# Second mixer's latent heads: values as the stationary operand, turned probabilities moving, two heads in two column strips

## What is computed

```python
q = (rmsnorm(c_q, q_norm) @ w_uq).reshape(B, S, H, MLA_NOPE + MLA_ROPE)     # H = 16, S = 256
kv = (rmsnorm(c_kv, kv_norm) @ w_ukv).reshape(B, S, H, MLA_NOPE + MLA_V)   # MLA_V = 64
...
    s = (einsum('bqhd,bkhd->bhqk', qn, k_nope)
         + einsum('bqhr,bkr->bhqk', qr, k_rope)) * scale
    p = jax.nn.softmax(jnp.where(kpos[None, :] <= qpos[:, None], s, NEG), axis=-1)
    o = einsum('bhqk,bkhd->bqhd', p, v)
return o.reshape(B, S, H * MLA_V) @ w_o
```

## Time and profile before

| what | us |
|---|---|
| median of three runs (lowest to highest) | 1389.64 (1388.46 to 1389.67) |
| the profiled execution's own time | 1388.37 |
| its span | 1386.6 |
| TensorE busy, DVE busy, ACT busy in the span | 1375.7, 901.8, 741.9 |
| granted clock of TensorE, mean | 0.998 |
| the latent heads, from the end of step 15's transposes to the first matmul of the projection | 630.4 to 654.5 |

### The profile page before, as it was taken

One profiled execution on the slowest core, in us unless ns is written; L12 is line 12 of the kernel. 1 busy time (PEld: TensorE's weight loads), 2 busy tenths in 40 slices (PEclk: granted clock), 3 DMA queues, 4 the chain that ended last, 5 costly groups with the idle time before them and its releaser, 6 DMA issues.

```text
span 1386.6 us, 21310 instructions
## 1 busy us (share of the span) xinstructions
PE 1375.7 (99%) x8246; PEld 1219.9 (88%) x8246; DVE 901.8 (65%) x1156; ACT 741.9 (54%) x921; POOL 60.8 (4%) x97
## 2 busy tenths in 40 slices
PE   9999999999999999999999999999999999999997
PEld 8999989888888888899888888888889999888886
DVE  6565798565566656776666667666657767666566
ACT  7566665343464444558554445545445467544444
POOL 1000010100010000010200000000000002100000
PEclk9999999999999999999999999999999999999999
DMA  9543432255455555561565554755555400555552
GB/s 373 183 173 122 174 131 92 91 209 202 154 183 187 201 187 182 180 210 37 209 249 182 189 203 155 272 182 182 183 199 194 153 32 5 224 184 195 197 182 91
DMA packets 34717, 240.16 MB, mean 173 GB/s; under 512 B 3994, under 2 KB 4138, under 8 KB 6880
## 3 DMA queue, kind: packets, MB, share of 16 engines
q1 hardware_dynamic: 32928, 232.50, 47.0%
q0 software_dynamic: 1296, 6.15, 1.2%
q10 hardware_dynamic: 432, 0.66, 0.1%
HBM read 237.16 MB, written 1.08 MB: 172 GB/s over the span
## 4 chain that ended last, share of the span: by engine, by line
PE 97%; DMA 1%; DVE 1%; ACT 1%; issue 0%; POOL 0%; POOLq 0%; ACTq 0%; DVEq 0%
PE ps L750 22%; PE ps L720 16%; PE ps L722 16%; PE ps L721 16%; PE ps L758 12%; PE ps L1056 3%; PE ps L1030 2%; PE ps L1040 2%; PE ps L1382 1%; DMA raw<-in_stream 1%; PE ps L3048 1%; PE ps L662 1%; PE ps L3054 1%; PE ps L3251 1%; PE ps L846 1%; PE ps L1376 0%
## 5 line engine op out<-in xcount | busy, mean ns | idle before, releaser
L427 DVE TENSOR_TENSOR low<-raw,high 128x2048 fp32r<-128x2048 f32 x210 | 478.6, 2281 | 230.0 <-ACT high L416 229.7
L416 ACT ACTIVATE high<-raw 128x2048 fp32r<-128x2048 f32 (+1 forms) x212 | 401.9, 1898 | 75.4 <-PE ps L722 70.6
L750 PE MATMUL ps<-nt,high 128*128 128x512 f32 x1344 | 319.9, 390 | 0.0
L750 PEld LDWEIGHTS ps<-nt,high 128*128 128x128 f32 x1344 | 249.0, 188 | 49.7
L758 PEld LDWEIGHTS ps<-nt,low 128*128 128x128 f32 x1344 | 167.5, 189 | 3.6
L758 PE MATMUL ps<-nt,low 128*128 128x256 f32 x1344 | 168.6, 283 | 0.0
L720 PE MATMUL ps<-high,hth 128*128 128x512 f32 x320 | 124.5, 389 | 0.0
L721 PE MATMUL ps<-low,hth 128*128 128x512 f32 x320 | 124.5, 389 | 0.0
L722 PE MATMUL ps<-high,htl 128*128 128x512 f32 x320 | 124.5, 389 | 0.0
L720 PE MATMUL ps<-nt,high 128*128 128x256 f32 x392 | 111.5, 285 | 0.0
L722 PE MATMUL ps<-nt,low 128*128 128x256 f32 x392 | 110.7, 282 | 0.0
(11 more groups left out here) (441 smaller groups left out, 1995.7 us busy)
## 6 DMA issues: line engine op xcount, KB each, us to landing
raw<-in_stream SPq DMA_DIRECT2D x214, 1024.0 KB, 4.8
late<-in_first SPq DMA_DIRECT2D x4, 512.0 KB, 5.7
late<-in_w POOLq DMA_DIRECT2D x1, 2048.0 KB, 11.3
scr<-bias_by_distance POOLq DMA_DIRECT2D x1, 2048.0 KB, 14.0
raw<-in_stream SPq DMA_DIRECT2D x2, 512.0 KB, 7.7
x<-in_x SPq DMA_DIRECT2D x1, 1024.0 KB, 11.9
scr<-in_mem SPq DMA_DIRECT2D x1, 1024.0 KB, 15.2
scr<-scr SPq DMA_DIRECT2D x8, 128.0 KB, 2.4
```

The costliest lines, as they stand in the source:

```text
L416: nc.scalar.activation(high_of(t, slice(0, n)), raw[t % SLOTS][:, 0:n], ACT.Copy).then_inc(w_high, 1)
L427: nc.vector.tensor_tensor(low_of(t, slice(0, n)), raw[t % SLOTS][:, 0:n], high_of(t, slice(0, n)).bitcast(F32), ALU.subtract).then_inc(w_l ...
L750: last = nc.tensor.matmul(r3(bank, 2), w[:, k, P * j:P * j + P], nt[:, :, k, :], start=first and k == 0, stop=not first and k == KC - 1, s ...
```

## The change

For the latent heads alone, and nowhere else:

- The product with the values is made for two heads together once for each pair (`values_by_features`, in even steps). The values of a head, 128 keys by 64 features without the column of ones, are stationary; the turned probabilities move, 256 columns for the first 128 keys and 128 columns for the second. The output has features on the partitions: the even head in partitions 0 to 63, the odd head in 64 to 127, so that the two heads take two column strips of the array. The turned blocks are put in another order in PSUM for that (`turned_probs_at`), and there are four buffers for the copies in place of two, since both heads of a pair have to be there.
- The sums come from the exponentials (`accum_out`). From the third pair on the exponentials wait for `at_read`, since there are three buffers of sums.
- DVE takes the reciprocal of the sums of a pair spread over 64 columns each, so of 128x256 elements with tokens on the partitions, into `ml_yt` (`at_shares`). TensorE transposes this in two blocks of 128x128, right behind the products of the pair. DVE then copies the turned shares from PSUM, and multiplies the output in PSUM with them into `ml_yt`.
- The transposes of `pe_y` fall away for these heads. `act_y` and `dve_y` read `ml_yt`.

```diff
+            def values_by_features(p):
+                for a in (2 * p, 2 * p + 1):
+                    pe.wait_ge(at_copied[a % 2], a // 2 + 1)
+                pe.wait_ge(at_read, 2 * (p - 1))
+                for kt in range(TT):
+                    for a in (2 * p, 2 * p + 1):
+                        half = slice(64 * (a % 2), 64 * (a % 2) + 64)
+                        last = nc.tensor.matmul(heads_out(p)[half, P * kt:S], UNITS[a]["v"][kt][:, 0:MLA_V],
+                                                ml_p[a % 4][:, S * kt:S + P * kt], start=kt == 0, stop=kt == 1,
+                                                skip_group_check=True)
+                last.then_inc(at_out, 1)
+                pe.wait_ge(at_shares, p - MLA0 // 2 + 1)
+                for t in range(TT):
+                    last = nc.tensor.transpose(heads_shares(p)[:, P * t:P * t + P], ml_yt[:, slot_of(p), P * t:P * t + P], ident)
...
+                last.then_inc(at_out, 1)
...
-                if first <= a - 3:
+                if first <= a - 3 and by_features(a - 3):
+                    if (a - 3) % 2:
+                        values_by_features((a - 3) // 2)
+                elif first <= a - 3:
                     values(a - 3)
...
+                    if by_features(a) and a >= first + RING:
+                        act.wait_ge(at_read, 2 * ((a - RING) // 2) + 2)
...
+                            last = nc.scalar.activation(at_s[b][:, c], src[:, c], ACT.Exp, scale=-1.0,
+                                                        bias=at_nm[r][:, t:t + 1],
+                                                        accum_out=at_sums[a // 2 % 3][:, at:at + 1])
...
+                if not odd and first <= a - 5 < first + n and by_features(a - 5):
+                    yt = ml_yt[:, slot_of(p - 1), :]
+                    dve.wait_ge(at_out, 2 * (p - 1) + 2)
+                    ch.link(nc.vector.tensor_copy(yt, heads_shares(p - 1)))
+                    nc.vector.tensor_tensor(yt, heads_out(p - 1), yt, ALU.mult).then_inc(at_read, 2)
...
+                if odd and by_features(a - 2) and first <= a - 2 < first + n:
+                    q = (a - 2) // 2
+                    if q - MLA0 // 2 >= 4:
+                        dve.wait_ge(turn_low, y_turned("mly", (q - MLA0 // 2 - 4) // 2))
+                    dve.wait_ge(at_exp, a - 1)
+                    nc.vector.reciprocal(ml_yt[:, slot_of(q), :].rearrange("p (t u d) -> p t u d", t=TT, u=2),
+                                         by_unit(at_sums[q % 3]).rearrange("p u t -> p t u").unsqueeze(3)
+                                         .broadcast_to([P, TT, 2, 64])).then_inc(at_shares, 1)
```

More of the change, by code:

```diff
@@ L931, in build, with by_features, slot_of, probs_at @@
         neg_sink = tiny(SW_H)
+        at_shares = s_("at_shares")
+        ml_p = [at_p[0], at_p[1], ml["y"][:, 1024:1536], ml["y"][:, 1536:2048]]
+        ml_yt = r3(ml["y"][:, 0:1024], 4)
+        def by_features(a):
+            return MLA0 <= a < MLA0 + MLA_H
+        def slot_of(p):
+            return (p - MLA0 // 2) % 4
+        def probs_at(a):
+            return ml_p[a % 4] if by_features(a) else at_p[a % 2]
+        def turned_probs_at(a, c):
+            return ((P, 2 * P, 0)[c // P] if by_features(a) else c)
+        def heads_out(p):
+            return ps[6 + p % 2][:, 0:S]
+        def heads_shares(p):
+            return ps[6 + p % 2][:, S:2 * S]
         def out_at(a):
@@ L974, in pe_y, with y_source @@
                 last.then_inc(turned, 1)
+        def y_source(name, b):
+            if name == "mly":
+                return ml_yt[:, 2 * (b % 2):2 * (b % 2) + 2, :]
+            return r3(y_bank(name, b), 2)
         def act_y(act, name, b):
-            act.wait_ge(turned, y_turned(name, b))
-            nc.scalar.activation(TURNS[name][3][:, 2 * b:2 * b + 2, :], r3(y_bank(name, b), 2), ACT.Copy)\
+            if name == "mly":
+                act.wait_ge(at_read, MLA0 + 4 * b + 4)
+            else:
+                act.wait_ge(turned, y_turned(name, b))
+            nc.scalar.activation(TURNS[name][3][:, 2 * b:2 * b + 2, :], y_source(name, b), ACT.Copy)\
                 .then_inc(turn_high, 1)
@@ L998, in pe_y_out @@
             pe_pair(pe, name, 0, 0, acts)
-            for c in (KC - 2, KC - 1):
+            for c in (KC - 2, KC - 1) if y == "nsy" else ():
                 heads_here(pe, y, c)
@@ L1073, in pe_units @@
                     ready[a - 3]()
-                if first <= a - 3:
+                if first <= a - 3 and by_features(a - 3):
+                    if (a - 3) % 2:
+                        values_by_features((a - 3) // 2)
+                elif first <= a - 3:
                     values(a - 3)
                 c, odd = divmod(a - (first + n - 2 * KC) - 7, 2)
-                if y and odd == 0 and 0 <= c < KC - 2:
+                if y == "nsy" and odd == 0 and 0 <= c < KC - 2:
                     heads_here(pe, y, c)
@@ L1083, in copy_probs @@
             eng.wait_ge(at_turned, a + 1)
-            if a >= 2:
+            if by_features(a):
+                eng.wait_ge(at_out, max(MLA0, 2 * (a // 2 - 2) + 1))
+            elif a >= 2:
                 eng.wait_ge(at_out, a - 1)
[L1086 to L1089, removed]
+            ins = nc.scalar.activation(probs_at(a)[:, 0:w], ps[2 + a % 2][:, 0:w], ACT.Copy)
             ins.then_inc(at_copied[a % 2], 1)
@@ L1171, in dve_units @@
                 ready = odd and first <= a - 4 < first + n
-                if ready:
+                if ready and by_features(a - 4):
+                    pass
+                elif ready:
                     inv = at_inv[p % 3]
@@ L1187, in dve_units @@
                     ch.mark(weigh(p, inv))
-                if not odd and first <= a - 5 < first + n:
+                if not odd and first <= a - 5 < first + n and not by_features(a - 5):
                     ch.join()
```

16 lines of the change are left out of this document (11 added, 5 removed).

## The result

The changed kernel takes **1398.01 us** (median of 6 runs, 1396.31 to 1398.69), the kernel before 1389.15 (6 runs, 1388.42 to 1389.84). The ratio is 1.0062, with an interval of 1.0052 to 1.0072: 8.6 us slower, 7.2 to 10.0. The forecast was 1394.4, +4.8. The profiled execution took 1398.69, its span 1396.9, 10.3 more than the 1386.6 before.

The account below looks back on a forecast made before the run. DVE was taken to bound the loop at 3.87 us a pair against TensorE's 3.16. A projection start 5.2 us later less 0.44 for dropped transposes gave +4.8, on the median 1389.64 so 1394.4 us; range 1392.0 to 1398.5.

Parts of the forecast that it names:

- The mechanism and its size: Latent heads' loop: DVE becomes the bound at 3.87 us a pair, with a wide reciprocal of 1.81 us.
- rival B: DVE's wide reciprocal is dearer than the slope, 2.16 us, because of a fixed start; +7.6, 1397.2 us; chance 0.12.
- TensorE's pair: TensorE's work for a pair in the loop: scores, turning, products 0.96 and shares 0.22, in all 3.16 us.
- Strips that take turns: Products of a pair on TensorE gain nothing if strips don't overlap; adds 8 x 0.2, so up to +6.5.
- In the two steps in which `dve_y` falls (23 and 27) 0.61 are added: DVE's work in the loop: each of these two steps takes 0.61 us more than a plain pair.
- the chain over TensorE's scores: The `at_read` wait, followed through ACT and TensorE to the next scores: ready at +5.05, 0.25 us before DVE asks.
- TensorE idle some 0.7 us for each pair: Sign expected in the profile after: TensorE idles this long in front of the turning and of the shares.
- A: The forecast itself: DVE bounds the loop at 6.2 to 7.0 ns an element; +4.2 to +5.8; chance 0.66.
- Rival C: DVE's wide reciprocal runs at a copy's pace, 0.4 us; TensorE bounds again and gains 2.2 us, 1387.4; chance 0.10.
- the walk: Followed DVE from head 15's scores to the loop's end: projection starts at 659.7 instead of 654.50, +5.2 us.

Follow-up runs that it names:

- waits filled: The changed kernel with eleven unused matmuls put in the three places where TensorE waits at the loop's end; 1395.32 us.
- both remedies: The changed kernel with exponentials waiting for the reciprocal instead of the evacuation, and eleven unused matmuls in TensorE's three waits at the loop's end; 1393.95 us.
- both parts: The changed kernel with exponentials waiting for the reciprocal instead of the evacuation, and the reciprocal taken of 4 sums, then spread by a copy; 1388.08 us.
- exponentials freed: The changed kernel with exponentials from the third pair on waiting for the reciprocal (at_shares) instead of the evacuation (at_read); 1394.62 us.
- shares first: The kernel with narrow reciprocal, spreading copy and exponentials waiting for the reciprocal, with a pair's shares' transposes moved in front of its products; 1390.77 us.
- the second attempt: Nine unused matmuls at the loop's end, four writing where head 14's turning writes: 1397.83 us in the changed kernel, 1395.49 with exponentials waiting for the reciprocal.

## Why the prediction was right, and where it was not

The 9.1 us fall into three parts, from four spans (before 1386.6, after 1395.7, waits filled 1393.5, both remedies 1391.4):

| part | us | from |
| --- | --- | --- |
| the change with its wide reciprocal, and no more | 4.8 | 1391.4 - 1386.6 |
| DVE's waits in the `y` steps | 2.1 | 1393.5 - 1391.4 |
| the clock at the loop's end | 2.2 | 1395.7 - 1393.5 |

The first part is a net: the rest of the change gives 1.3 back (both parts, 1385.3), so the wide reciprocal in place of the narrow one and its copy costs 6.1. The other two parts depend on their order: with the exponentials freed first they are 2.9 and 1.4. Each figure is from one execution. Counted from the turning of head 13 to the first projection matmul, as the prediction did (24.4 before, 29.6 forecast), the stage takes 32.6 us after, 31.5 with the waits filled and 29.6 with both remedies.

- **The mechanism and its size: right.** DVE is the bound of the loop, busy 3.68 us of a plain pair's 3.78. The reciprocal took 1.75 (1.81 forecast), the pair 3.78 (3.87), and with copy and narrow reciprocal the loss is gone. The slope between two small sizes held to a size sixteen times larger; rival B's fixed start, which would have made it 2.16, is out. The Trainium skill (VectorE: DVE Perf Modes, section Walkthrough: the 8-slice pipeline in each mode) states a repeat count of 8 for a reciprocal's divide, from which the prediction estimated 8.3 ns an element; the trace doesn't agree with that estimate, with 6.2.
- **TensorE's pair: right.** 3.14 us in the kernel with both parts, 3.16 forecast. The products with both changes of mode were put at 0.96; they are 0.80, and the shares behind them are 0.37 instead of 0.22, together 0.95. Strips that take turns are excluded by 0.80 against 1.44.
- **Term mis-sized: "In the two steps in which `dve_y` falls (23 and 27) 0.61 are added".** It was 1.80. 0.86 is left with the exponentials freed (4.64 - 3.78): 0.73 from the step's start to the reciprocal, which waits for the step's end (`turn_low`), where the 0.61 was read in front of an evacuation that doesn't; and 0.12 in front of the step, of which it isn't shown whether it is its own or still ACT's. The other 0.94 is the wait. The prediction named what the `at_read` wait holds up on ACT, the exponentials and the next copy, but followed only the chain over TensorE's scores, where 0.25 us were left. `act_y` stands in the same queue, and in these two steps DVE waited for it, 0.99 us each.
- **Missed: the clock.** "TensorE idle some 0.7 us for each pair" stood in the prediction, and its consequence didn't. In the middle of the loop that idle time cost no clock (18.15 busy of 22, granted 1.00); with the waits at the end, 1.42 of 4, it did in the profiled execution, and the projection paid for part of it: its first six matmuls took 664.23 to 666.79, 2.56 us instead of 1.39. The sum had no term for the clock, which put it at nothing.
- **Compensations.** The pair was 0.09 shorter than taken, five times 0.45; the `y` steps' own price was 0.25 higher, twice 0.5. So it is luck that the 4.8 of the first part agrees to the tenth. One bound was added up wrong: strips that take turns, 1.6 us on top of A's +5.8, give +7.4 and not +6.5. It didn't come to bear, since the strips overlap.
- **Rival C** (reciprocal at a copy's pace, 1387.4) is what the kernel with both parts does: 1388.08, 1.3 us under before by corrected span, where C had 2.2. The pair's gain is there, 0.34 us; what it lacked is the end of the loop, where ACT's copies and not DVE bound. The -0.44 inside the projection was not in C either.
- **The range** held the time (1392.0 to 1398.5, measured 1398.01), but its upper end stood for a dearer reciprocal, and what brought the time 3.6 us above the forecast was two effects that no rival had. That it still held is owed to the width of the range, not to the walk.

What stays open: what makes the clock fall at 605 us in some executions and not in others. TensorE has no gap there; right before it stand 20 matmuls of a single column (2.1 us). Filling waits has nothing to fill there, and nothing was tried. Open too is what decides at the loop's end: the waits have to do with it, since none of the ten executions with filled waits has so low a mean clock, but the clock stayed up around 1.97 busy of 4 us in one kernel (shares first), and in one execution of the second attempt.

## What to carry to other kernels

An operation that is free at 4 elements a partition is not free at 256: before a broadcast is moved into an instruction, take the price per element of that instruction from two sizes in the trace, and compare it with a copy (here 1.75 us against 0.17 + 0.29). Where a wait is added, walk through everything queued behind it on that engine, the rare steps too, since each has its own consumer with its own slack. And when TensorE starts to wait, look at the granted clock of what comes next: a stage that ends with gaps can hand a slow array to the following one, and a few unused matmuls in the waits can be worth more than they cost. Look at several executions, since one may lose the clock and the next not.

## What the runs showed of the hardware

- A float32 reciprocal on DVE costs 6.2 ns for each element of a partition from 16 to 256 elements (0.254 and 1.75 us); a copy from SBUF that spreads 4 values over 256 elements takes 0.29 us in all.
- Two column strips of 64 run at the same time even when their matmuls are queued as four and four (0.81 us), not only in alternation (0.80); one strip alone takes 1.44.
- Changing between the whole array and strips costs about 0.09 us on the way in (the first product starts 0.20 behind the last transpose, where transposes stand 0.11 apart; no run isolates this one) and 0.15 to 0.20 on the way back (shares 0.37 for 0.22, scores 0.85 for 0.65). The Trainium skill (TensorEngine Tiling (Array Packing), section Key Properties) says that a change of mode drains the engine, and these delays agree with it.
- The granted clock can halve behind a partly idle stretch in which no single wait is over 1.22 us: it did around 1.42 busy of 4 us and 2.19 of 4, and not around 3.47 of 4, nor around 1.97 of 4 in another kernel. Once down it stayed so for 3.4 or 6.8 us here, though TensorE was busy again.
- The clock differs between executions of one program: 3.4 us at the lower level at 605 us or none, with TensorE busy throughout (5 of 5 us in both traces), 1.2 us in the time.
